# Single transpositions between projection products in the attention stages of a three-layer block

## The reference

```python
# A: qkv = h @ w_qkv (1024 x 9216): 3 dilations x 16 heads x 64; per dilation a masked softmax
# B: qkv = h @ w_qkv (1024 x 3072): 16 heads, causal softmax over 256 tokens
# C: proj = h @ w_in: 8 heads with forget gates, plus a convolution and a pooling branch
q = apply_partial_rope(rmsnorm(qkv[:, :, 0], q_gain), cos, sin)   # A, B; C without rope
k = apply_partial_rope(rmsnorm(qkv[:, :, 1], k_gain), cos, sin)
p = softmax(where(mask, q @ k.T * scale, -inf))
x = x + (p @ v) @ w_o
x = x + (silu(gate(conv3(h @ w_up))) * val(conv3(h @ w_up))) @ w_down
```

## Time and profile before

| what | value |
|---|---|
| median of 3 runs | 1024.45 us (1023.81 to 1024.62) |
| span of the profiled execution, first to last instruction | 1023.2 us |
| median less that span: what lies around it | 1.25 us |
| PE busy | 1018.9 us, 100% |
| PEld busy | 960.4 us, 94% |
| DVE, ACT, POOL busy | 86%, 67%, 34% |
| granted TensorE clock, mean | 1.000 |

### The profile page before, as it was taken

The page is one execution under the profiler, slowest core; times in us unless marked ns, Lnnn a source line. Parts: engine busy times, 40 slices in busy tenths (PEclk is TensorE's granted clock), DMA queues, the critical chain, the costliest instruction groups (busy, mean ns, idle before and its releaser), DMA issues.

```text
span 1023.2 us, 22239 instructions
## 1 busy us (share of the span) xinstructions
PE 1018.9 (100%) x8026; PEld 960.4 (94%) x8026; DVE 880.5 (86%) x1535; ACT 687.1 (67%) x1267; POOL 349.1 (34%) x370
## 2 busy tenths in 40 slices
PE   9999999999999999999999999999999999999998
PEld 9999999999999999999999999999998999999998
DVE  7977778787799988887888999988897879999886
ACT  7776766766766665677786766656697776665663
POOL 5312221112255533342111556433350025654332
PEclk9999999999999999999999999999999999999999
DMA  9744465556476666526364566666544536666651
GB/s 318 256 152 151 144 186 155 159 175 205 149 236 195 219 188 202 170 94 217 126 192 153 185 206 213 199 194 193 157 123 135 166 125 213 219 206 195 196 163 42
DMA packets 57753, 183.40 MB, mean 179 GB/s; under 512 B 6352, under 2 KB 9680, under 8 KB 57424
## 3 DMA queue, kind: packets, MB, share of 16 engines
q1 hardware_dynamic: 56816, 181.52, 55.8%
q10 hardware_dynamic: 864, 0.92, 0.3%
HBM read 181.36 MB, written 1.05 MB: 178 GB/s over the span
## 4 chain that ended last, share of the span: by engine, by line
PE 99%; DMA 0%; DVE 0%; ACT 0%; DVEq 0%; issue 0%
PE ps L455 23%; PE ps L457 12%; PE ps L714 10%; PE ps L716 10%; PE ps L715 9%; PE ps L1902 6%; PE ps L1903 6%; PE ps L1904 6%; PE ps L1363 2%; PE ps L1365 2%; PE ps L1364 2%; PE ps L640 1%; PE ps L911 1%; PE ps L806 1%; PE ps L949 1%; PE ps L894 1%
## 5 line engine op out<-in xcount | busy, mean ns | idle before, releaser
L423 DVE TENSOR_TENSOR w_lo<-w_raw,w_hi 128x1024 fp32r<-128x1024 f32 (+2 forms) x369 | 441.2, 1213 | 31.9 <-ACT w_hi L415 31.5
L415 ACT ACTIVATE w_hi<-w_raw 128x1024 fp32r<-128x1024 f32 (+2 forms) x369 | 353.5, 972 | 121.7 <-PE ps L457 102.4
L455 PE MATMUL ps<-xg,w_hi 128*128 128x512 f32 x1056 | 362.8, 390 | 0.0
L457 PE MATMUL ps<-xg,w_lo 128*128 128x256 f32 x1056 | 291.5, 276 | 0.0
L455 PEld LDWEIGHTS ps<-xg,w_hi 128*128 128x128 f32 x1056 | 198.2, 188 | 38.7
L2027 POOL TENSOR_TENSOR prob_t<-prob_t,qkT 128x256 f32<-128x256 f32 x63 | 111.1, 1763 | 257.2 <-ACT prob_t L1948 257.2
L457 PEld LDWEIGHTS ps<-xg,w_lo 128*128 128x128 f32 x1056 | 198.2, 188 | 0.1
L714 PE MATMUL ps<-w_hi,xg 128*128 128x384 f32 (+1 forms) x556 | 192.5, 346 | 0.0
L716 PE MATMUL ps<-w_hi,xg 128*128 128x384 f32 (+1 forms) x556 | 187.3, 337 | 0.0
L715 PE MATMUL ps<-w_lo,xg 128*128 128x384 f32 (+1 forms) x556 | 185.7, 334 | 0.0
L1902 PE MATMUL ps<-g_hi,w_hi 128*128 128x256 f32 x528 | 146.0, 276 | 0.0
(11 more groups left out here) (196 smaller groups left out, 1382.0 us busy)
## 6 DMA issues: line engine op xcount, KB each, us to landing
w_raw<-w_stream SPq DMA_DIRECT2D x228, 512.0 KB, 3.8
w_raw<-w_stream SPq DMA_DIRECT2D x137, 384.0 KB, 3.6
w_raw<-w_stream SPq DMA_DIRECT2D x4, 392.0 KB, 3.1
con<-consts SPq DMA_DIRECT2D x1, 1024.0 KB, 6.8
x_all<-x_t SPq DMA_DIRECT2D x4, 256.0 KB, 5.1
conv_taps<-taps SPq DMA_DIRECT2D x1, 1024.0 KB, 7.2
w_raw<-w_stream SPq DMA_DIRECT2D x4, 192.0 KB, 4.5
x_all<-x_a SPq DMA_DIRECT2D x3, 256.0 KB, 5.6
```

Source lines behind the costliest of these rows:

```text
L415: nc.scalar.activation(w_hi[s][:, 0:w], w_raw[s][:, 0:w], ACT.Copy).then_inc(w_hi_done, 1)
L423: nc.vector.tensor_tensor(w_lo(c)[:, 0:w], w_raw[s][:, 0:w], w_hi[s][:, 0:w].bitcast(F32), ALU.subtract).then_inc(w_lo_done, 1)
L455: nc.tensor.matmul(bank(b, 0, 2 * TOK), w_hi[s][:, k * P:(k + 1) * P], xg[:, k, :, :].rearrange("p h t -> p (h t)"), start=(k == 0), stop= ...
L457: last = nc.tensor.matmul(bank(b), w_lo(c)[:, k * P:(k + 1) * P], xg_hi[:, k, :], start=False, stop=(k == KT - 1), skip_group_check=True)
```

## The change

In the steady parts of the loops the transpositions are handed to `unit_chunk_pe` as a function `beside`. From the sixth of the chunk's 12 products on, one step of it is issued after each product: the waits and the first transposition after product 6, one after each product up to product 11 (6 steps) or 9 (4 steps). The signal on the last transposition of a group stays on that one. All conditions are the same as before, in the same order, and no instruction is added or removed. The first queries of stage A and the ends of the three stages still call whole groups.

```diff
-    def unit_chunk_pe(eng, st, n):
+    def unit_chunk_pe(eng, st, n, beside=None):
...
+        def product(out, x, w, step, start, stop):
+            last = nc.tensor.matmul(out, x, w, start=start, stop=stop)
+            if beside is not None and step >= 0:
+                beside(step)
+            return last
...
             for t in range(2):
...
-                nc.tensor.matmul(out, hi, wh, start=(k == 0), stop=False)
-                nc.tensor.matmul(out, hi, wl, start=False, stop=False)
-                last = nc.tensor.matmul(out, lo, wh, start=False, stop=(k == KT - 1))
+                step = 6 * kk + 3 * t - 5
+                product(out, hi, wh, step, k == 0, False)
+                product(out, hi, wl, step + 1, False, False)
+                last = product(out, lo, wh, step + 2, False, k == KT - 1)
...
+    def turn_one(role, i):
+
+        t, g = divmod(i, NDIL)
+        return nc.tensor.transpose(bank(Q_BANK, g * TOK + t * P, P), qn(0, role, t)[:, g * P:(g + 1) * P],
+                                   con[:, CON_ID:CON_ID + P])
+
+    def qt_step(eng, pr, i):
+        if i == 0:
+            qt_wait(eng, pr)
+        if i < 2 * NDIL:
+            one = turn_one(0, i)
+            if i == 2 * NDIL - 1:
+                one.then_inc(att[0].qt, 1)
...
+    def prob_t_a_step(eng, pr, qt, i):
+
+        a, per = att[0], 2 + qt
+        if i == 0:
+            eng.wait_ge(a.pn, 2 * pr + qt + 1)
+        if i < 2 * per:
...
+    def prob_t_step(eng, st, pr, i):
...
     def att_a_pe(eng):
         for n in range(N_A):
             p, o = divmod(n, 3 * UCH)
-            unit_chunk_pe(eng, 0, n)
+            beside = None
+            if o == 0 and p > 0:
+                beside = lambda i: kt_step(eng, p - 1, i)
+            if o in (5, 6) and p > 0:
+                beside = lambda i: prob_t_a_step(eng, p - 1, o - 5, i)
+            if o == 9 and p > 0:
+                beside = lambda i: qt_step(eng, p, i)
+            unit_chunk_pe(eng, 0, n, beside)
...
     def att_b_pe(eng):
...
+            if o == 0 and p >= 3:
+                beside = lambda i: prob_t_step(eng, 1, p - 3, i)
+            if o == 3 and p >= 1:
+                beside = lambda i: qkt_step(eng, 1, p - 1, i)
+            unit_chunk_pe(eng, 1, n, beside)
...
     def att_c_pe(eng):
...
+            if o == 0 and p >= 3:
+                beside = lambda i: prob_t_step(eng, 2, p - 3, i)
+            if o == 3 and p >= 1:
+                beside = lambda i: qkt_step(eng, 2, p - 1, i)
+            unit_chunk_pe(eng, 2, n, beside)
```

More of the change, by code:

```diff
@@ L752, in mix_place, with qt_wait @@
         return x.rearrange("p (l t r) -> p t r l", t=2, r=CLASSES // 2)
-    def qt_pe(eng, pr):
+    def qt_wait(eng, pr):
         a = att[0]
@@ L758, in qt_pe, with kt_wait @@
         past(eng, a.ptr, 2 * pr, 0, None)
[L759 to L765, removed]
+    def kt_wait(eng, pr):
         a = att[0]
@@ L768, in kt_pe @@
         eng.wait_ge(a.qe, pr + 1)
[L769 to L773, removed]
-    def qkt_pe(eng, st, pr):
[L777 to L795, removed]
+    def turn_one(role, i):
+        t, g = divmod(i, NDIL)
+        return nc.tensor.transpose(bank(Q_BANK, g * TOK + t * P, P), qn(0, role, t)[:, g * P:(g + 1) * P],
+                                   con[:, CON_ID:CON_ID + P])
@@ new lines, in qt_step, with kt_step, qt_pe @@
+    def qt_step(eng, pr, i):
[5 more added lines that the diff above has]
+                one.then_inc(att[0].qt, 1)
+    def kt_step(eng, pr, i):
+        if i == 0:
+            kt_wait(eng, pr)
+        if i < 2 * NDIL:
+            one = turn_one(1, i)
+            if i == 2 * NDIL - 1:
+                one.then_inc(att[0].kt, 1)
+    def qt_pe(eng, pr):
+        for i in range(2 * NDIL):
+            qt_step(eng, pr, i)
@@ new lines, in kt_pe, with qkt_step @@
+    def kt_pe(eng, pr):
+        for i in range(2 * NDIL):
+            kt_step(eng, pr, i)
+    def qkt_step(eng, st, pr, i):
+        a = att[st]
+        if i == 0:
+            if st == 1:
+                eng.wait_ge(a.rope, pr + 1)
+            else:
+                eng.wait_ge(a.nm, 2 * (pr + 1))
+                if pr in (0, 2):
+                    eng.wait_ge(side_lo, pr + 2)
+            past(eng, a.qe, pr, 0, None)
+            past(eng, a.ke, pr, 0, None)
+            if st == 1 and pr == 0:
+                eng.wait_ge(rest_in, 32)
+            if pr - 2 >= FIRST_QUARTERS[st]:
+                eng.wait_ge(pv_sum, summed(st, pr - 2))
+            else:
+                past(eng, a.olo, pr - 1, 0, None)
+        if i < 4:
+            role, t = divmod(i, 2)
+            order = CON_SWAP if (role, t) == (1, 0) else CON_ID
+            one = nc.tensor.transpose(bank(Q_BANK + role, t * P, P), qn(st, role, t)[:, role * P:(role + 1) * P],
+                                      con[:, order:order + P])
+            if i == 3:
+                one.then_inc(a.qt, 1)
@@ L797, in block_scores @@
+    def qkt_pe(eng, st, pr):
+        for i in range(4):
+            qkt_step(eng, st, pr, i)
     def block_scores(st, q, kk, whole):
@@ L902, in score_a_pe @@
         classes(1).then_inc(a.score, 1)
-    def prob_t_a_pe(eng, pr, qt):
[L906 to L912, removed]
+    def prob_t_a_step(eng, pr, qt, i):
+        a, per = att[0], 2 + qt
+        if i == 0:
+            eng.wait_ge(a.pn, 2 * pr + qt + 1)
+        if i < 2 * per:
+            h, n = divmod(i, per)
+            o = (3 * qt + n) * P
+            one = nc.tensor.transpose(bank(SA_BANK + 2 * qt + h, n * P, P), prob[h][:, o:o + P], con[:, CON_ID:CON_ID + P])
+            if i == 2 * per - 1:
+                one.then_inc(a.pt, 1)
+    def prob_t_a_pe(eng, pr, qt):
+        for i in range(2 * (2 + qt)):
+            prob_t_a_step(eng, pr, qt, i)
     def pv_a_pe(eng, pr):
@@ L936, in pv_a_pe @@
         last.then_inc(a.pv, 1)
-    def prob_t_pe(eng, st, pr, g):
[L940 to L950, removed]
+    def prob_t_step(eng, st, pr, i):
+        a = att[st]
+        if i == 0:
+            eng.wait_ge(a.pn, 2 * pr + 2)
+            if pr == 0:
+                eng.wait_ge(rest_in, 32)
+        if i < 6:
+            h, n = divmod(i, 3)
+            o, order = (prob_part(st, 0, 0)[0], prob_part(st, 1, 0)[0], prob_part(st, 1, 0)[0] + P)[n], (CON_ID, CON_SWAP, CON_SWAP)[n]
+            one = nc.tensor.transpose(bank(S_BANK + h, n * P, P), prob[h][:, o:o + P], con[:, order:order + P])
+            if i == 5:
+                one.then_inc(a.pt, 1)
+    def prob_t_pe(eng, st, pr, g):
+        for i in range(6):
+            prob_t_step(eng, st, pr, i)
     FIRST_QUARTERS = (None, 0, 1)
@@ L1407, in att_a_pe @@
             p, o = divmod(n, 3 * UCH)
-            unit_chunk_pe(eng, 0, n)
+            beside = None
[6 more added lines that the diff above has]
+            unit_chunk_pe(eng, 0, n, beside)
             if n == 7:
                 cols_pe(eng, 0)
-            if o == 0 and p > 0:
-                kt_pe(eng, p - 1)
             if o == 1 and p > 0:
@@ L1416, in att_a_pe @@
                 pv_a_pe(eng, p - 2)
-            if o in (5, 6) and p > 0:
-                prob_t_a_pe(eng, p - 1, o - 5)
             if o == 7 and p == PAIRS_AB - 1:
                 pv_a_pe(eng, p - 1)
-            if o == (9 if p > 0 else 11):
-                qt_pe(eng, p)
+            if n == 11:
+                qt_pe(eng, 0)
         p = PAIRS_AB - 1
@@ L1544, in att_b_pe @@
             p, o = divmod(n, UCH)
-            unit_chunk_pe(eng, 1, n)
+            beside = None
+            if o == 0 and p >= 3:
[3 more added lines that the diff above has]
+            unit_chunk_pe(eng, 1, n, beside)
             if p == 0 and o == 3:
                 cols_pe(eng, 2)
-            if o == 0 and p >= 3:
-                prob_t_pe(eng, 1, p - 3, 0)
             if o == 1 and p >= 2:
@@ L1553, in att_b_pe @@
                 pv_quarters_pe(eng, 1, p - 3)
-            if o == 3 and p >= 1:
-                qkt_pe(eng, 1, p - 1)
         p = PAIRS_AB - 1
@@ L1682, in att_c_pe @@
             p, o = divmod(n, UCH)
-            unit_chunk_pe(eng, 2, n)
+            beside = None
+            if o == 0 and p >= 3:
[3 more added lines that the diff above has]
+            unit_chunk_pe(eng, 2, n, beside)
             if n == 1:
@@ L1691, in att_c_pe @@
                 ln_var_pe(eng)
-            if o == 0 and p >= 3:
-                prob_t_pe(eng, 2, p - 3, 0)
             if o == 1 and p >= 2:
@@ L1703, in att_c_pe @@
                 pw_pe(eng)
[L1704 to L1709, removed]
         p = PAIRS_C - 1
```

## The result

| | median of 20 runs each | range |
|---|---|---|
| before | 1024.43 us | 1023.75 to 1024.77 |
| after | 1025.70 us | 1025.28 to 1026.27 |

The ratio is 1.0013, with a 95% interval of 1.0007 to 1.0019: 1.27 us more. That is within the 0.2% named as the bound of no change. The interval leaves out 1.0000 all the same: the change costs about a thousandth.

A forecast was written before the change was run, and what follows sets the result against it. TensorE's back-to-back instructions were taken to bound the kernel. From 1024.45 us, +1.1 for lone transpositions and +0.5 for stalls gave +1.6, 1026.05 us, no change within 0.2%; range 1023.4 to 1028.6.

The forecast's parts named there:

- The bound: All three attention stages: TensorE's instructions one behind the other set the time, PE busy for the whole span.
- What was costed at nothing: Earlier group signals to ScalarE and VectorE, chunk-finished signals up to 0.6 us later, and transfers: no cost to PE.
- The lone one's price: A single transposition between two products costs 0.115 us, priced like the last of a group; 26.45 us for 230.
- The border term: 230 moved transpositions cost 26.45 us alone against 25.3 us in groups: 1.1 us more.
- The stalls: First queries and keys of stage B stall about 0.4 us, first keys of A about 0.1; together 0.5 us.
- the moved wait of the probabilities: Rival: probabilities of B and C stall if VectorE's weighting comes 0.9 us later against PE; 1028.2 us, chance 0.06.
- The faster rival: Next product's load hides under the product ahead, so a lone transposition costs 0.058 us; 1013 us, chance 0.07.
- The load's time as the price: A lone transposition costs only its weight load, 0.107 us anywhere; 24.6 us in all, a gain of 0.7.
- The slower rival: Products behind each lone transposition go on losing a little, 0.126 us each; 1028.6 us, chance 0.27.

The follow-up runs named there:

- experiment 1: Changed kernel, but first keys of stage A and first queries and keys of stage B stay whole groups behind their chunk; 1025.41 us, ratio 1.0009.
- experiment 4: Kernel before plus unread extra matmuls of 128, 64 or 32 columns, alone or grouped, between products in seven pairs of stage B; 1032.83 us, single run.
- experiments 3 and 6: 3: changed kernel, two transpositions behind every second product, 1025.98 us; 6: kernel before, stage A's two probability groups as one of ten, 1024.43 us.
- experiment 5: Changed kernel with lone transpositions at the chunk's end, behind products 7 to 12 or 9 to 12; 1025.22 us, ratio 1.0010.

## Why the prediction was right, and where it was off

The forecast was 1.6 us more, 1026.05; measured 1.27 more, 1025.70, inside the range and inside no change.

- **The bound.** TensorE back to back: right. PE is busy for 100% of the span on the page of the kernel before and of the kernel after, and apart from the two stalls the loss is read from distances between starts on PE. What was costed at nothing stayed there: PE lists no new wait for ScalarE, VectorE or a transfer.
- **The lone one's price.** 0.115 forecast from the last of a group, 0.114 measured between lone ones. In part this is luck. Read over whole chunks, by the starts in nanoseconds (a chunk without transpositions takes 2.080 us in both kernels), the last of six costs 0.115 and the last of four 0.126, while lone ones cost 0.113 to 0.114 each. So a lone one is not simply the last of a group; reading only up to the second product hid the difference.
- **The border term, +1.1.** The sign was right and the size was not: 0.70 by the stretch of four pairs. The term is a difference of two sums of some 25 us, made from rows with two decimals. Over whole chunks the groups of before cost 0.660 and 0.453, not 0.657 and 0.447, since the products behind a group go on losing a little; spread out, six cost 0.680 and four 0.461. So 27 x 0.020 + 17 x 0.008 = 0.68, in line with the 0.70.
- **The stalls, +0.5.** Right in both places and in size: 0.38 and 0.13 by distances (forecast 0.4 and 0.1), and experiment 1, which removes these two waits, agrees with 0.45. No other group waits, so the moved wait of the probabilities did not come, as the spare time in the earlier trace rows had it.
- **The faster rival.** A lone one that costs its columns only: disproved by experiment 4, where 32 columns cost as much as 128. The reason against it from the load rows held: the load behind a lone transposition starts with it. The other reason, that the transposition streams as long as a product of twice its width, was beside the point: a rounded matmul of 128 columns has a record of 0.22 instead of 0.27, and the same slot. The Trainium skill, "TensorE: Matmul & The Clock Gate", section "Step-by-step: what each phase is for", describes a window that pulls loads ahead of running matmuls; in these traces no load of a 128 x 128 operand starts before the matmul ahead of its own.
- **The load's time as the price.** The rows have 0.109 inside a group and 0.114 alone, so spreading out brought no gain. The Trainium skill, "TensorE: Matmul & The Clock Gate", section "LDWEIGHTS (loading the stationary operand)", gives a load as its columns over 1.2 GHz, 107 ns for 128. The 0.11 between the starts of two loads agrees; the estimate from it, a gain of 0.7 us, did not come.
- **The slower rival.** Every border at 0.126: not so in the steady state, as 0.2875 between lone ones shows, not 0.30. Its thought, that products go on losing a little behind a transposition, does show in small: in stage A, in the pairs, at the chunk's end and behind the group of ten, by about 0.03 per pair of heads. (The price from which this rival decides comes out of the sum given there as 26.85 / 230 = 0.1167, not 0.1174; the 0.114 measured is under both.)

Not settled: what makes these last nanoseconds. A border is not a fixed price for each meeting (experiments 3 and 6), and it depends on the place (experiment 5). A cause was not found: it is 0.1 us in a stretch of 121, and no experiment here separates one.

## What to carry to other kernels

In this kernel a matmul with a 128 x 128 load of its own costs the slot of that load, 0.11 us, alone or in a group and with 32 columns as with 128; spreading such matmuls out among long products hid nothing. When a step is moved earlier, look at the first turn of each loop and not only at the steady ones: here 2 of 44 groups came too late for it, and both were first turns. And read a small difference from one long stretch at both kernels, not as the difference of two large sums.

## What was not expected of the hardware

- The slot of a lone matmul is the same with 32, 64 and 128 columns, 0.11 to 0.115 us, while its record falls from 0.22 to 0.18: so the length of a record did not tell here what an instruction costs.
- Pairs were no cheaper than single ones, 0.114 each, though the inner distance is 0.109: the last of a pair pays 0.119.
- The price of a border hangs on the place: later in the chunk it rose in stage A and fell in stage B, and behind the group of ten a whole chunk without transpositions ran 0.013 us longer.
- A stall of 0.13 us left no line with an engine's name among the waits, and one of 0.38 a line of 0.2, because the running matmul's record covers the gap.
